# FFN gate and up as one level of Strassen's seven products, and the down projection row by row

## The reference

```python
for l in range(DEPTH):            # DEPTH = 2, D_MODEL = 1024, D_FF = 2816, SEQ = 512
    x = x + 0.5 * swiglu(rms_norm(x, g_ffn1[l]), w_ffn1_gate[l], w_ffn1_up[l], w_ffn1_down[l])
    h = rms_norm(x, g_mix[l])
    x = x + (conv_gating_mixer(h, ...) if l % 2 == 0 else stick_breaking_mixer(h, ...))
    x = x + 0.5 * swiglu(rms_norm(x, g_ffn2[l]), w_ffn2_gate[l], w_ffn2_up[l], w_ffn2_down[l])
return rms_norm(x, g_final)
# swiglu(h, w_gate, w_up, w_down) = (silu(h @ w_gate) * (h @ w_up)) @ w_down
```

## Time and profile before

| | |
|---|---|
| median of 3 runs | 1992.18 us (1991.56 to 1993.14) |
| profiled execution, first to last instruction | 1989.1 us |
| PE busy | 1936.5 us, 97% |
| DVE, ACT, POOL busy | 923.1, 608.8, 391.4 us |
| memory traffic | 173.74 MB, mean 87 GB/s |

### The profile page before, as it was taken

One profiled execution on the slowest core, in us unless ns is written; L12 is line 12 of the kernel. 1 busy time (PEld: TensorE's weight loads), 2 busy tenths in 40 slices (PEclk: granted clock), 3 DMA queues, 4 the chain that ended last, 5 costly groups with the idle time before them and its releaser, 6 DMA issues.

```text
span 1989.1 us, 22688 instructions
## 1 busy us (share of the span) xinstructions
PE 1936.5 (97%) x8611; PEld 1587.0 (80%) x8611; DVE 923.1 (46%) x849; ACT 608.8 (31%) x636; POOL 391.4 (20%) x375
## 2 busy tenths in 40 slices
...
GB/s 129 106 105 84 99 88 87 107 104 66 43 85 85 105 85 105 73 93 109 104 86 105 85 85 90 99 107 84 43 43 43 43 85 106 84 105 83 83 93 80
DMA packets 314908, 173.74 MB, mean 87 GB/s; under 512 B 6172, under 2 KB 305760, under 8 KB 314864
## 3 DMA queue, kind: packets, MB, share of 16 engines
...
q0 software_dynamic: 128, 0.07, 0.0%
q10 hardware_dynamic: 112, 0.03, 0.0%
...
## 4 chain that ended last, share of the span: by engine, by line
PE 84%; DVE 8%; POOL 4%; ACT 2%; issue 1%; DMA 0%; SPq 0%; DVEq 0%; POOLq 0%; ACTq 0%
PE ps L289 27%; PE ps L290 27%; PE ps L291 27%; DVE y L1114 4%; POOL ssq L1381 2%; POOL sq L1379 1%; DVE w_lo L1009 1%; PE ps L660 1%; PE ps L654 1%; ACT w_hi L774 1%; DMA x_tok<-in_x_dram 0%; PE ps L396 0%; DVE rinv L1032 0%; DVE u L1208 0%; DVE g_buf L1217 0%
## 5 line engine op out<-in xcount | busy, mean ns | idle before, releaser
L289 PE MATMUL ps<-xg_hi,w_hi 128*128 128x512 f32 x1632 | 640.5, 392 | 11.6 <-DVE w_lo L1009 11.6
L290 PE MATMUL ps<-xg_lo,w_hi 128*128 128x512 f32 x1632 | 637.0, 390 | 0.0
L291 PE MATMUL ps<-xg_hi,w_lo 128*128 128x512 f32 x1632 | 636.8, 390 | 0.0
L1009 DVE TENSOR_TENSOR w_lo<-stage,w_hi 128x2048 fp32r<-128x2048 f32 (+1 forms) x180 | 389.1, 2162 | 405.8 <-ACT w_hi L767 324.7
L289 PEld LDWEIGHTS ps<-xg_hi,w_hi 128*128 128x128 f32 x1632 | 307.9, 189 | 77.2 <-issue 13.7
L290 PEld LDWEIGHTS ps<-xg_lo,w_hi 128*128 128x128 f32 x1632 | 307.7, 189 | 64.5 <-issue 1.2
L291 PEld LDWEIGHTS ps<-xg_hi,w_lo 128*128 128x128 f32 x1632 | 307.5, 188 | 64.5
L289 PE MATMUL ps<-hid_hi,w_hi 128*128 128x512 f32 x704 | 279.3, 397 | 0.0
L290 PE MATMUL ps<-hid_lo,w_hi 128*128 128x512 f32 x704 | 279.1, 396 | 0.0
L291 PE MATMUL ps<-hid_hi,w_lo 128*128 128x512 f32 x704 | 279.1, 396 | 0.0
L1389 POOL TENSOR_TENSOR hid_lo<-up,hid_hi 128x512 f32 x88 | 114.1, 1297 | 833.8 <-ACT hid_hi L797 833.8
...
## 6 DMA issues: line engine op xcount, KB each, us to landing
...
```

What stands on the lines that cost most here:

```text
L289: pe.matmul(to, a_hi, b_hi, start=start, stop=False, skip_group_check=True)
L290: pe.matmul(to, a_hi, b_lo, start=False, stop=False, skip_group_check=True)
L291: return pe.matmul(to, a_lo, b_hi, start=False, stop=stop, skip_group_check=True)
L1009: dve.tensor_tensor(w_lo[:, slot, 0:cols], stage[:, slot, 0:cols], w_hi[:, slot, 0:cols].bitcast(F32), ALU.subtract).then_inc(w_lo_made, 1)
```

## The change

Gate and up are now worked out by steps over pairs of hidden tiles f and f + 11. In a step the weights are a 2 x 2 block matrix (rows in two halves of four tiles, columns f and f + 11), and x is one too (feature halves and token halves). Strassen's scheme in Winograd's form needs seven products for the four output blocks: seven items of 1024 weight columns (gate and up, four row tiles each), each with 24 matmuls of 256 columns, 168 in a step, and there are 11 steps in each FFN. Two weight sums (`T1`, `T3`) are made by DMAs from POOL's queue that add to what a first load put there, two (`T2`, `T4`) by POOL instructions. The sums of x are made once for each FFN (`x_sum`, `x_pair`), on pairs of tiles k and k + 4; DVE and ACT make them and their high and low parts. Three copies (ACT) and five sums (DVE) take the seven products out of four banks in each step. Weights of an item stand in one of four ring slots.

Down is a loop over 22 rows: a row is 1024 weight columns and one hidden tile, 8 banks x 3 = 24 matmuls with 512 columns, and all eight banks stay open. Only the last two rows (three in FFN 1, `TAIL`) go bank by bank, so the eight outputs end there one behind the other. The scaling of the hidden tile by 1/rms, and its high and low part, are made for each row. The first four items of a step 0 run over three of the four pairs of x and then over the last one. In the core of the diff below the indentation is cut; before each step of the loop, SP waits until the item's old weights are split.

```diff
...
+ITEMS = 7
+W11, W21, T1, T3, T2, W22, T4 = range(ITEMS)
+PART_OF = [0, 1, 4, 3, 5, 6, 2]
...
+BANK_OF = [0, 1, 2, 3, 0, 2, 3]
+RING = 4
+TAIL = [2, 3, 2, 2]
+OUT_ORDER = [IN_ORDER, PAIRED, IN_ORDER, IN_ORDER]
...
+xs_hi = sb("xs_hi", [P, 7, KH, HS], F32R, ffn_scope)
+xs_lo = sb("xs_lo", [P, 7, KH, HS], F32R, ffn_scope)
+sums = sb("sums", [P, 3, 1024], scope=ffn_scope)
...
+    copies = sb("copies", [P, 4, 2, HS], scope=gate_scope)
...
+h_split = sb("h_split", [P, 4, 2, S], F32R, ffn_scope)
...
+def load_step(n, step):
+    lo0 = n * FFN_ITEMS - ITEMS
+    sp.wait_ge(item_lo_made, step.count(ITEMS, lo0 + W11 + 1))
+    load_raw(n, W11, step, 0, 0)
+    sp.wait_ge(item_lo_made, step.count(ITEMS, lo0 + W21 + 1))
+    sp.wait_ge(t4_made, step.count(1, n * HF))
+    load_raw(n, W21, step, KH, 0)
+    sp.wait_ge(item_lo_made, step.count(ITEMS, lo0 + T1 + 1))
+    sp.wait_ge(t2_made, step.count(1, n * HF))
+    load_raw(n, T1, step, 0, 0)
+    sp.wait_ge(item_lo_made, step.count(ITEMS, lo0 + T3 + 1))
+    load_raw(n, T3, step, 0, HF)
+    sp.wait_ge(item_lo_made, step.count(ITEMS, lo0 + W22 + 1))
+    load_raw(n, W22, step, KH, HF)
...
+def gate_part(n, item, bank, ks):
...
+    for part in range(2):
+        for k in ks:
...
+            mm = three(pe, ps[:, bank + BANK_OF[item], part * HS:(part + 1) * HS], w_hi[:, slot, cols],
+                       w_lo[:, slot, cols], xs_hi[:, PART_OF[item], k, :], xs_lo[:, PART_OF[item], k, :],
+                       start=(item < 4 and part == 0 and k == 0))
...
+def gate_first(n):
+    norm, step = NORM_FFN[n], Step(0)
+    for item in range(4):
+        pe.wait_ge(item_lo_made, n * FFN_ITEMS + item + 1)
+        for k in range(KH - 1):
+            pe.wait_ge(xs_lo_made, 8 * n + 2 * k + (1 if item < 2 else 2))
+            gate_part(n, item, 0, [k])
+    for item in range(4):
+        pe.wait_ge(xs_lo_made, 8 * n + 2 * (KH - 1) + (1 if item < 2 else 2))
+        gate_part(n, item, 0, [KH - 1]).then_inc(item_used, 1)
+    gate_rest(n, step, T2)
+    pe.wait_ge(ssq_added, (norm + 1) * DT)
+    sum_squares().then_inc(ssq_summed, 1)
+    gate_rest(n, step, W22)
+    gate_rest(n, step, T4)
+    pe.wait_ge(rms_made, norm + 1)
+def gate_step(n, step):
...
+    last_rows = range(FT - TAIL[n], FT)
+    for at in range(DT):
+        for d in last_rows:
+            if at == 0:
+                pe.wait_ge(item_lo_made, n * FFN_ITEMS + GATE_ITEMS + d + 1)
+                pe.wait_ge(hid_lo_made, n * FT + d + 1)
+            mm = down_part(n, d % 4, (DOWN_AT[n] + d) % RING, at, OUT_ORDER[n][at], False)
+        mm.then_inc(down_summed, 1)
+        if n == 3 and at == 5:
+            pe.wait_ge(x_ready, NORM_FINAL * DT + 4)
+            for j in range(4):
+                turn_result(j, range(TT))
...
+def gate_step(n, step):
+    if step.i is not None or step.f:
+        silu(n, Step(step.f - 1, step.i))
+    hi(n, step, T2)
+    copy_v0(n, step)
+    hi(n, step, W22)
+    hi(n, step, T4)
+    copy_r0(n, step)
+    hi(n, step.next(), W11)
+    copy_v(n, step)
+    if step.i is None and step.f == 0:
+        token_rms(NORM_FFN[n])
+    hi(n, step.next(), W21)
+    hi(n, step.next(), T1)
+    hi(n, step.next(), T3)
...
+def gate_step(n, step):
+    c11(n, step)
+    lo(n, step, W22)
+    lo(n, step, T4)
+    s57(n, step)
+    lo(n, step.next(), W11)
+    c22(n, step)
+    lo(n, step.next(), W21)
+    c12(n, step)
+    c21(n, step)
+    if step.i is None and step.f == 0:
+        invert_rms(NORM_FFN[n])
+    scale_gate(n, step)
+    lo(n, step.next(), T1)
+    lo(n, step.next(), T3)
+    make_hid(n, step)
+    lo(n, step.next(), T2)
...
+def x_sum(n, k):
...
+    dve.wait_ge(x_ready, pair_ready(n, k)[1])
+    if n or k:
+        dve.wait_ge(xs_lo_made, 8 * n + 2 * k)
+    dve.tensor_tensor(x_sums[:, 0, :], x1a, x1b, ALU.subtract).then_inc(x_sums_made, 1)
+    dve.wait_ge(x1b_scaled, KH * n + k + 1)
+    dve.scalar_tensor_tensor(x_sums[:, 1, :], x2b, g2, rms[:, (k % 2) * HS:(k % 2 + 1) * HS],
+                             ALU.mult, ALU.subtract).then_inc(x_sums_made, 1)
+    dve.wait_ge(x_sums_made, made + 2)
+    dve.scalar_tensor_tensor(x_sums[:, 2, :], x1a, g1, x_sums[:, 1, :], ALU.mult, ALU.add).then_inc(x_sums_made, 1)
+    dve.wait_ge(x_sums_made, made + 3)
+    dve.scalar_tensor_tensor(x_sums[:, 3, :], x2a, n2, x_sums[:, 2, :], ALU.mult, ALU.add).then_inc(x_sums_made, 1)
...
+def x_pair(n, k):
...
+    x_sum(n, k)
+    dve.wait_ge(xs_hi_made, made + 1)
+    dve.scalar_tensor_tensor(xs_lo[:, NEG_X1A, k, :], x_res[:, k, 0:HS], n1, xs_hi[:, NEG_X1A, k, :].bitcast(F32),
+                             ALU.mult, ALU.subtract)
+    dve.wait_ge(xs_hi_made, made + 2)
+    dve.scalar_tensor_tensor(xs_lo[:, X2A:X2B + 1, k, :], x_res[:, k + KH, :].rearrange("p (h c) -> p h c", h=2), g2,
+                             xs_hi[:, X2A:X2B + 1, k, :].bitcast(F32), ALU.mult, ALU.subtract).then_inc(xs_lo_made, 1)
+    dve.wait_ge(xs_hi_made, made + 3)
+    dve.scalar_tensor_tensor(xs_lo[:, PART_S3, k, :], x_sums[:, 0, :], g1, xs_hi[:, PART_S3, k, :].bitcast(F32),
+                             ALU.mult, ALU.subtract)
+    dve.wait_ge(xs_hi_made, made + 4)
+    dve.wait_ge(x_sums_made, made + 4)
+    dve.tensor_tensor(xs_lo[:, PART_S1:, k, :], x_sums[:, 1:4, :], xs_hi[:, PART_S1:, k, :].bitcast(F32),
+                      ALU.subtract).then_inc(xs_lo_made, 1)
...
+    elif n == 1:
+        for k in range(3):
+            residual(n, 2 * k)
+            residual(n, 2 * k + 1)
+            x_pair(2, k)
+        lo(2, first, 0)
+        residual(n, 6)
+        residual(n, 7)
+        for item in range(1, 4):
+            lo(2, first, item)
+        x_pair(2, 3)
...
+def add_w12(n, step):
+    pool.wait_ge(raw_loaded[T1], step.count(32, raw_count(n, T1) + 32))
+    for part, w in enumerate(ffn_weights[n][:2]):
+        pool.dma_start(raw(T1)[:, part * 512:(part + 1) * 512].rearrange("p (k f) -> p k f", k=KH),
+                       rows_of(w, 0, KH, bass.ds(step.count(P, HF * P), P)), accum_op=ALU.add).then_inc(t1_made, 16)
...
+def add_t2(n, step, first=False):
+    pool.wait_ge(t1_made, step.count(32, n * HF * 32 + 32))
+    pool.wait_ge(raw_loaded[W22], step.count(32, raw_count(n, W22) + 32))
+    if not first:
+        pool.wait_ge(item_lo_made, step.count(ITEMS, n * FFN_ITEMS - ITEMS + T2 + 1))
+    pool.tensor_tensor(raw(T2), raw(T1), raw(W22), ALU.add).then_inc(t2_made, 1)
+def add_t4(n, step, first=False):
+    pool.wait_ge(t2_made, step.count(1, n * HF + 1))
+    pool.wait_ge(raw_loaded[W21], step.count(32, raw_count(n, W21) + 32))
+    if not first:
+        pool.wait_ge(item_lo_made, step.count(ITEMS, n * FFN_ITEMS - ITEMS + T4 + 1))
+    pool.tensor_tensor(raw(T4), raw(T2), raw(W21), ALU.add).then_inc(t4_made, 1)
...
+def squares(norm, order, next_ffn):
+    for at, j in enumerate(order):
+        square_tile(j, norm * DT + at + 1)
+        if next_ffn is not None and at == 1:
+            add_w12(next_ffn, Step(0))
+            add_w22(next_ffn, Step(0))
+        elif next_ffn is not None and at == 5:
+            add_t2(next_ffn, Step(0), True)
+            add_t4(next_ffn, Step(0), True)
...
```

More of the change, by code:

```diff
@@ new lines, in gate_rest @@
+            def gate_rest(n, step, item):
+                pe.wait_ge(item_lo_made, step.count(ITEMS, n * FFN_ITEMS + item + 1))
+                if item == T2:
+                    pe.wait_ge(v0_copied, step.count(1, n * HF + 1))
+                elif item == W22:
+                    pe.wait_ge(r0_copied, step.count(1, n * HF + 1))
+                elif item == T4:
+                    pe.wait_ge(evicted, step.count(EVICTS, n * HF * EVICTS + 2))
+                gate_part(n, item, step.bank(), range(KH)).then_inc(item_used, 1)
```

743 lines of the change are left out of this document (509 added, 234 removed).

## The result

The changed kernel takes 2055.69 us (median of 4, 2051.74 to 2057.78) against 1992.34 for the kernel before beside it (4 runs): ratio 1.032, 95% interval 1.0305 to 1.0334. It is 63 us slower; 47 were forecast. The profiled execution has a span of 2056.1 us.

The account below looks back on a forecast made before the run. PE, busy 97% of the span, was taken as the bound, with its waits at stage borders. Terms: -64 + 75.5 + 3 + 17.6 + 10.4 + 5 = +47.5, so 1992.2 + 47 = 2039 us; own range 2015 to 2065, overall 1960 to 2100.

Parts of the forecast that it names:

- the mechanism of the borders: Between stages: DVE instructions with two SBUF operands and POOL instructions take turns, each waiting for the other's current one.
- 64 - 3 = 61: Gate and up: 40 loop steps at 20.16 instead of 21.76 us save 64; the first steps add 3.
- I take no wait: Gate and up loop: after a step's last product, 3 us of DVE work fit the 5.7 us before PE wants T1.
- rival B: Loop not bound by PE: DMA engines full, or late T2 and T4 block DVE, 1 us a step; 2087 us, chance 0.17.
- +0.7 each: First steps of the FFNs: the reciprocal ahead of T1's low part makes 6.5 us against 5.7; +3 in all.
- +75.5: Step 0 of the four FFNs, preparing x in turns with POOL: +19.5, +17, +20 and +19 us; bounds 15 and 90.
- The row by which I chose: Evidence against free slipping in at the borders: each low part of x lasted double while POOL worked.
- rival A: Borders: turns cost DVE less since its short instructions slip in; step 0 costs 15, a mixer 3; 1967 us, chance 0.24.
- +8.8 each: First chunk of both mixers: PE waits for the sum of squares, no longer hidden; +17.6 us together, bounds 3 and 10 each.
- The clock's term: Six borders with an idle pause, then PE at 1.2 instead of 2.4 GHz: 0.8 us each, +5, upper end +10.
- another pace as a sign of being wrong: Down: 0.2343 us a matmul and no change in time; the prediction is wrong if the pace isn't 0.234.
- The end: After FFN 3's down: squares delay the last norm, +9.5 to +10.4 us, 10.4 taken; 20 us from last bank to end.

Follow-up runs that it names:

- experiment 5: The changed kernel with POOL's weight sums T2 and T4 over 16 of 1,024 columns, the rest a constant: 2008.8 us, ratio 1.0095 to the kernel before.
- experiment 6: The changed kernel with its adding DMAs made plain copies of the same bytes, so sums T1 and T3 are left out: 2031.35 us, ratio 1.0213.
- experiment 1: The changed kernel with POOL's squares and their sums on 16 instead of 512 columns, norms' factor not computed: 1984.45 us, ratio 0.9964.
- experiment 8: Against the changed kernel: ACT squares, PE sums FFN norms' squares, POOL adds the other norms', reciprocal one item earlier in step 0: 1989.68 us, ratio 1.0004.
- experiment 3: The changed kernel with ACT making the squares and POOL only adding them: 2015.89 us, ratio 1.0125.

## Why the prediction was right, and where it was too low

The sign and the mechanism of the borders held; the 63 us lie in the range given for the forecast itself. Gate and up cost 20 us more than forecast: the loop and the first steps are 25 over it, the borders 4 under.

- **Pace and loop.** Undisturbed the pace is 0.119 a matmul, 19.94 a step against 20.16: the floor was forecast 0.22 too high. (The Trainium skill, page "TensorE: Matmul & The Clock Gate", section "Back-to-back issue gap", has a formula for a single matmul that gives 109 ns for 256 columns and 216 for 512; the trace has 119 and 232, with a weight load for each matmul.) The 36 later steps average 20.52, since T2 and T4 block DVE. With the first steps, the 40 steps gave 36 us back, where 64 - 3 = 61 were forecast. "I take no wait" was the step that failed, and rival B had its mechanism (T2 and T4 late by the adding DMA, meeting the scaling and T1's low part) at 1 us a step; the size is 0.59 (experiments 5 and 6). The DMA engines aren't full: an adding byte costs 2.4 times a plain one (18.1% of the engines against 7.5% for the same 46.22 MB) and the loop runs at PE's floor at a share of 0.90. But T2 starts 2.5 us later behind its first issue than with copies, and POOL's issues last 1.3 to 2.2 us in the trace (in part beside one another), not 0.55 as taken from the earlier trace rows.
- **The first steps.** +0.7 each was forecast; they take 24.3 three times and 22.2, against 20.98 without the sums. With the reciprocal alone they would have taken 20.98 (+1.04, not +0.7); T2 and T4 in the same stretch make the rest, 11 us in all, with some matmuls at the low clock behind PE's waits.
- **Turns and borders.** Step 0 ends at 69.1 (forecast 68.7), 42.2 (41), 42.2 (42.4) and 44.4 (45) us; +75.5 was forecast, and +72 is what the stages show, as the kernel before lost 3 us more ahead of FFN 3 than I took (its first two tiles there took 28.9 us and not 25.7). Experiments 1 and 8 show the cause, though experiment 3 gave back less than the turns account for. The row by which I chose, instructions lasting as long as their neighbour, decided against rival A; its 1967 would have needed borders 15 us shorter each.
- **The mixers and the clock.** +8.8 each was forecast. The wait is 9.1 us, about as sized, but the stages grow by 12.2 and 17.3; without POOL's squares they are back to +0.8 and +3.5 of before (these two stay unexplained). So squares cost 11.4 and 13.8. What goes beyond the wait is mostly the low clock behind it: 1.8 us in each sum of squares, and 1.4 and 2.6 us in the 7 and 13 matmuls that follow. The clock's term, 5 us for six pauses, was too small. The mean granted clock is 0.988 before and 0.956 after, that is 2 x 0.012 x 1989 = 48 us at 1.2 instead of 2.4 GHz before and 2 x 0.044 x 2056 = 181 after, PE's idle time included. As an estimate of its price I took from the timelines the matmuls of 256 and 512 columns that start at about twice their spacing without a wait: 51 before and 258 after, 9.5 and 31 us over the normal spacing. With the sums of squares that is some 25 us more, and not 5. A short wait can be enough: PE waited for 2.6 us until 1028.8, the starts went to 0.21 at 1030.1 and stayed there for 3.4 us.
- **Down and the end.** The pace of down fell from 0.2343 to 0.2324, some 1 us a stage; I had taken none, and had named another pace as a sign of being wrong. Why it fell wasn't tested. The end costs 5.7 instead of 10.4, and from the last down matmul it is 12.4 us and not 20: PE's transposes and its waits for the scaled x (3.0 us) now stand ahead of the last two banks.
